# The first branch gate of the second block one attention step later

## What is computed

```python
for l in range(2):
    x = x + 0.5 * swiglu(rms(x, ffn1_norm), wg1, wu1, wd1)
    h = rms(x, mix_norm)
    (q_a, g_a, kc, vc, ks, vs, kw, vw, q_b, k_b, v_b, gate_a, gate_b) = split(h @ w_in)
    y_a = nsa(q_a, g_a, kc, vc, ks, vs, kw, vw, ...) @ w_branch_nsa    # 8 heads
    y_b = moba(q_b, k_b, v_b) @ w_branch_moba                          # 8 heads
    merged = sigmoid(gate_a) * y_a + sigmoid(gate_b) * y_b
    x = x + merged @ w_out
    x = x + 0.5 * swiglu(rms(x, ffn2_norm), wg2, wu2, wd2)
return rms(x, final_norm)
```

## Time and profile before

| | |
|---|---|
| median of 3 runs | 1896.64 us (1894.64 to 1898.02) |
| the profiled execution | 1895.2 us, its span 1893.4 us |
| PE matmul, busy | 1849.8 us, 98% |
| DVE busy | 1270.3 us, 67% |
| ACT busy | 1084.1 us, 57% |
| POOL busy | 95.9 us, 5% |
| mean granted TensorE clock | 0.998 of full speed |
| DMA | 285.40 MB, 151 GB/s |

### The profile page before, as it was taken

The page is one execution under the profiler, slowest core; times in us unless marked ns, Lnnn a source line. Parts: engine busy times, 40 slices in busy tenths (PEclk is TensorE's granted clock), DMA queues, the critical chain, the costliest instruction groups (busy, mean ns, idle before and its releaser), DMA issues.

```text
span 1893.4 us, 33080 instructions
## 1 busy us (share of the span) xinstructions
PE 1849.8 (98%) x12748; PEld 1596.1 (84%) x12748; DVE 1270.3 (67%) x2139; ACT 1084.1 (57%) x1899; POOL 95.9 (5%) x83
## 2 busy tenths in 40 slices
PE   7999999999999999999999999999999999999998
PEld 5878878868788987888889988889888889998887
DVE  6663344477735569775677687767776677687765
ACT  5372264385726477774556567755774555567762
POOL 0000000004000005000000010000000000010001
PEclk9999999999999999999999999999999999999999
DMA  9232243232224213555532445545554542345443
GB/s 352 90 112 89 89 158 110 90 134 90 90 89 161 96 68 142 191 190 192 199 134 96 150 177 180 197 179 183 194 179 177 225 156 90 123 178 188 178 179 132
DMA packets 42565, 285.40 MB, mean 151 GB/s; under 512 B 4944, under 2 KB 6352, under 8 KB 9424
## 3 DMA queue, kind: packets, MB, share of 16 engines
q1 hardware_dynamic: 40832, 278.24, 40.4%
q0 software_dynamic: 1616, 5.52, 0.9%
HBM read 282.69 MB, written 1.05 MB: 150 GB/s over the span
## 4 chain that ended last, share of the span: by engine, by line
issue 49%; PE 41%; DVE 3%; POOL 3%; ACT 2%; DMA 1%; SPq 0%; DVEq 0%; POOLq 0%; ACTq 0%
PE bank L2211 7%; PE bank L2212 7%; PE bank L2213 7%; PE bank L2217 6%; PE bank L2218 3%; PE bank L2452 3%; PE bank L2422 2%; PE bank L2397 2%; POOL work L852 1%; PE bank L2313 1%; DVE panels_lo L1451 1%; DMA token_major<-weights 1%; POOL xT L895 1%; ACT work L1059 1%; ACT panels_hi L926 0%
## 5 line engine op out<-in xcount | busy, mean ns | idle before, releaser
L2217 PE MATMUL bank<-acts,panels_hi 128*128 128x512 f32 x2032 | 718.2, 399 | 3.5 <-DVE xT L1949 2.6
L1451 DVE TENSOR_TENSOR panels_lo<-raw_panels,panels_hi 128x1024 fp32r<-128x1024 f32 x468 | 577.8, 1252 | 186.6 <-ACT panels_hi L926 184.9
L926 ACT ACTIVATE panels_hi<-raw_panels 128x1024 fp32r<-128x1024 f32 x468 | 484.2, 1054 | 253.9 <-PE bank L2213 145.5
L2218 PE MATMUL bank<-acts,panels_lo 128*128 128x256 f32 x2032 | 569.4, 280 | 0.0
L2217 PEld LDWEIGHTS bank<-acts,panels_hi 128*128 128x128 f32 x2032 | 382.3, 188 | 98.1 <-DVE xT L1949 2.8
L2218 PEld LDWEIGHTS bank<-acts,panels_lo 128*128 128x128 f32 x2032 | 384.0, 189 | 0.2
L2211 PE MATMUL bank<-acts,panels_hi 128*128 128x256 f32 (+1 forms) x1112 | 349.5, 314 | 2.9 <-ACT gates L1403 1.2
L2212 PE MATMUL bank<-acts,panels_hi 128*128 128x256 f32 (+1 forms) x1112 | 344.3, 310 | 0.0
L2213 PE MATMUL bank<-acts,panels_lo 128*128 128x256 f32 (+1 forms) x1112 | 344.3, 310 | 0.0
L2211 PEld LDWEIGHTS bank<-acts,panels_hi 128*128 128x128 f32 x1112 | 211.8, 190 | 20.3 <-issue 3.9
L2213 PEld LDWEIGHTS bank<-acts,panels_lo 128*128 128x128 f32 x1112 | 211.9, 191 | 11.1
(11 more groups left out here) (282 smaller groups left out, 1961.0 us busy)
## 6 DMA issues: line engine op xcount, KB each, us to landing
raw_panels<-weights SPq DMA_DIRECT2D x252, 1024.0 KB, 4.8
token_major<-weights SPq DMA_DIRECT2D x4, 1024.0 KB, 8.7
near_bias<-rpb POOLq DMA_DIRECT2D x16, 256.0 KB, 3.4
xT<-xin SPq DMA_DIRECT2D x4, 512.0 KB, 5.9
gates<-weights SPq DMA_DIRECT2D x2, 1024.0 KB, 10.4
near_bias<-weights SPq DMA_DIRECT2D x4, 512.0 KB, 7.1
token_major<-weights SPq DMA_DIRECT2D x2, 512.0 KB, 12.8
out<-xT SPq DMA_DIRECT2D x4, 256.0 KB, 2.4
```

Source lines behind the costliest of these rows:

```text
L926: act.activation(slot_hi(n, a, b), raw_of(n, a, b), ACT.Copy).then_inc(hi_ready, 1)
L1451: dve.tensor_tensor(slot_lo(n, a, b), raw_of(n, a, b), slot_hi(n, a, b).bitcast(F32), ALU.subtract).then_inc(lo_ready, 1)
L2217: pe.matmul(bank.rearrange("p (c t) -> p c t", c=2), whi_, with_rest(xhi_), start=start, stop=False, skip_group_check=True)
L2218: return pe.matmul(bank[:, 0:T], wlo_, xhi_, start=False, stop=stop, skip_group_check=True)
```

## The change

The slot of gate 0 goes from step 0 to step 1; the other seven stay. Gate 0 is then issued on TensorE behind the scores of step 1 in place of those of step 0, and what hangs on its slot (its scaling, the roundings and splits of panel 2) moves by one step as well. Nothing is added or removed.

```diff
-GATE_SLOTS = (0, 2, 4, 6, 8, 10, 12, 14)
+GATE_SLOTS = (1, 2, 4, 6, 8, 10, 12, 14)
```

## The result

| | before | changed |
|---|---|---|
| median of 10 runs | 1896.56 us | 1903.41 us |
| lowest to highest | 1893.06 to 1900.37 | 1897.92 to 1906.96 |
| ratio to before | | 1.0033, 95% interval 1.0023 to 1.0043 |
| the profiled execution | 1895.2 us, span 1893.4 | 1904.96 us, span 1903.2 |

What follows compares the result with a forecast made beforehand. PE, busy 98% of the span, was taken as the bound, so only its holes could change: 1.21 + 1.72 = 2.93 us per layer, 5.9 in two, giving 1901.1 (profiled) or 1902.5 (median); range 1899.0 to 1905.0.

Steps and rivals of the forecast that it cites:

- Part 1: PE's hole ahead of gate 0 goes, since scores(1) fill it: 0.61 us gained per layer.
- Part 2: Ahead of gate 1, PE waits 1.82 us for DVE's scaling of gate 0: net loss 1.21 us, hole's gain included.
- Part 3: Inside gate 2, PE waits 1.72 us for DVE's split of panel 2's second half.
- Part 4: Loads of panels 3 and 4 and all later steps: no third wait, nothing given back, later starts move by 2.93 us.
- The sum: Both attention loops: 1.21 + 1.72 = 2.93 us in one layer, 5.9 us in two.
- C: Rival: TensorE's clock falls in the new waits, about 1.5 us a fall; one gives 1904.0, four 1908.5; 5%.
- A: Rival: only the first wait, ahead of gate 1, comes: +1.21 us twice, 1899.1; 8%.
- B: Rival: the gain alone, -0.61 us per layer, 1895.4, if DVE's chain to the scaling is 1.8 us shorter; 5%.

Runs made afterwards that it cites:

- scale first: The changed kernel, but DVE scales gate 0 ahead of normalise(1) in step 2, not behind it; ratio to before 1.0013.
- split behind scale: The changed kernel, but DVE splits panel 1's second half behind the scaling of gate 0 in step 2, not ahead of normalise(1); ratio to before 1.0024.
- late split only: The kernel before, with only the roundings and splits of panel 2 one step later, as in the changed kernel; ratio to before 1.0018.
- both repairs: The changed kernel with gate 0 scaled ahead of normalise(1) and panel 2 rounded and split in the old steps; ratios to before 0.9991 and 0.9990.
- neighbours in MoBA: The changed kernel with gates in slots 1, 3, 5, 7, 9, 10, 12, 14, so gates 4 and 5 are neighbours; ratio to before 1.0060.
- all odd slots: The changed kernel with gates in slots 1, 3, 5, 7, 9, 11, 13, 14; ratio to before 1.0050.
- waits filled: The changed kernel with idle matmuls on PE in the two waits, 12 ahead of gate 1 and 11 inside gate 2; ratio to before 1.0029.

## Why the prediction was right

**Part 1, the hole that goes.** Right. Gate 0 starts 988.89 - 986.50 = 2.39 us after scores(0) with no wait; the repaired kernels keep 0.62 per layer.

**Part 2, the wait ahead of gate 1.** Right to 0.01, in each link of the chain: from scores(0), DVE's normalise(0), max(1), split, normalise(1) and scaling start at 5.38, 6.95, 8.15, 9.28 and 11.13 us, where 5.38, 6.95, 8.15, 9.29 and 11.13 were summed. From scores(0) to gate 1 are 998.37 - 986.50 = 11.87, before 993.22 - 982.55 = 10.67: a net loss of 1.20 where 1.21 was summed. The profile calls the wait 1.65 and the prediction 1.82, since the prediction counts from the time at which PE could have started and the profile from the end of the busy time of the matmul ahead. The cause given, normalise(1) ahead of the scaling, is shown by scale first. What the chain left out is that the panel split in it is half covered by ScalarE's exponentials, as split behind scale showed; it changed nothing in the sum, because in the changed kernel the split is the later of the two, by 0.55.

**Part 3, the wait inside gate 2.** Right to 0.07. From gate 1 to values(1) are 1016.97 - 998.37 = 18.60, before 1010.03 - 993.22 = 16.81: 1.79 where 1.72 was summed. Late split only shows that it needs no other cause.

**Part 4, what costs nothing.** Right: no third wait came, for the load of panel 4 or anything else, and nothing was given back; the stretches of two layers make up the measured 6.3 within its interval.

**The sum.** 5.9 forecast, 6.0 in the traces, 6.3 by the ratio (4.4 to 8.2). That the profiled execution came out at 1904.96, near the top of the range, is chance: its clock fell mostly at places outside the loop. Two of the prediction's own signs didn't come as written. PE's busy time wasn't as it was but 4.7 us longer (0.9 of it is what the waits cost beyond their idle time), and one stretch had a granted clock under 1.00, which was a sign for C.

**The rivals.** A (only the first wait) falls with late split only and with the trace. B (the gain alone) describes what both repairs make of the change; its condition, DVE's chain shorter by 1.8 us, is just what moving one 0.7 us instruction ahead of a 1.85 us group brings about. C, the clock, was priced well at 1.5 us a fall (1.36 measured) and probably weighed too low: I gave 5% to it as a case, where it comes in part of the executions; by one fall in 18 waits, some one in five. The argument that a wait of 1.80 had cost nothing took one sample for a rule. In the changed kernel's profile the same wait, which the change doesn't touch, has this behind it:

```profile
495.00:498.00 3.00, 1.20 (x10) 0.48 (x6) 3.00 (x5) 2.46 (x6) 0.00 (x0) 1.00 0.00 0
498.00:502.00 4.00, 4.00 (x20) 2.81 (x19) 2.62 (x8) 3.29 (x8) 0.00 (x0) 0.57 0.80 264
```

The Trainium skill, "TensorE: Matmul & The Clock Gate" (Part 1: The HAM clock gate), says that the gate halves the clock after idle time; of the 18 waits here the trace agrees behind one, at 0.54 granted, and shows no fall behind the others.

## What to carry to other kernels

When one item of a hand-ordered pipeline moves by one step, list everything that hangs on the same index, on every engine, and for each follow the consumer's engine to its wait and the producer's engine to its signal; here the moved matmuls gained 0.6 us and two followers on DVE cost 1.8 us each. Two uses of one buffer in neighbouring steps leave only the work between them as cover; here it paid to put the item that frees the buffer at the head of its engine's step. Sum such a chain only where there is a row for every item of every engine in it: so it held to 0.01 us, and where an item of ScalarE was left out it missed. Measure such a thing in the trace between two fixed instructions: without a fall of the clock between them it resolved 0.02 us, where ten runs resolved 2.

## What the runs showed of the hardware

Whether a wait of TensorE lowers its clock isn't settled by its length: behind 1.65 us it fell once and stayed once in the same execution, with neighbours in MoBA it fell to 0.50 for 3 us behind a wait of 2.56 and stayed at 1.00 behind the 2.57 of the other layer, and in the kernel with all odd slots it fell behind a wait of 3.14 in the first layer and not behind the equal one in the second:

```profile
1069.80:1073.00 3.20, 0.09 (x2) 0.00 (x1) 3.03 (x6) 2.70 (x4) 0.00 (x0) 1.00 0.00 0
1073.00:1077.00 4.00, 3.97 (x22) 4.00 (x23) 3.63 (x4) 2.04 (x3) 0.00 (x0) 0.62 0.34 102
...
1656.00:1659.00 3.00, 0.15 (x4) 0.00 (x0) 2.77 (x5) 2.25 (x4) 0.00 (x0) 1.00 0.00 0
1659.00:1663.00 4.00, 3.71 (x31) 3.74 (x32) 3.88 (x5) 1.93 (x3) 0.00 (x0) 1.00 0.30 92
```

One fall cost 1.3 to 1.5 us between fixed instructions (1.36, 1.50 and 1.31 in these three kernels).

A matmul that begins an accumulation in one half of a PSUM bank, while another is open in the other half, costs the open one its partial sum: with the flags the output of waits filled was off by a relative error of 0.12, without them whole. The two kernels differ in the flag that ends an accumulation as well, so the runs alone show it for the pair of flags. The Trainium skill, "PSUM — Partial Sum Buffer" (The four PSUM rules), says the same: the flag acts on the whole bank, and two accumulations open at once in it can't both use it.
